# All eight heads of the second attention between the gating unit's tiles, and the gates in four wide groups

## What is computed

```python
h = rms_norm(x, norm_g)
q, k, v, z_a, u_b, v_b, z_b, g_a, g_b = split(h @ w_in)   # 7 x 1024 columns, then 2 x 2048
q, k = rms_norm(q per head), rms_norm(k per head)         # 8 heads of 128
att = causal softmax attention(q, k, v)                   # all 256 tokens are one block
y_a = (att * silu(z_a)) @ w_proj_a
mixed = w_s @ rms_norm(gelu(v_b) per head) + b_s          # 8 groups of 128, chunks of 128 tokens
y_b = (gelu(u_b) * mixed * silu(z_b)) @ w_proj_b
out = x + (sigmoid(g_a) * y_a + sigmoid(g_b) * y_b) @ w_out
```

## Time and profile before

| what | us |
|---|---|
| median of 3 runs | 1755.94 (1755.17 to 1756.29) |
| the profiled execution, its own time | 1755.48 |
| its span, first to last instruction | 1753.7 |
| u's and z_b's tiles, z_a's tiles with four heads, narrow gates with four heads | 1255.9 to 1452.8 |
| three wide gate groups | 1452.8 to 1576.7 |

### The profile page before, as it was taken

How to read it: one execution, slowest core, us unless ns; L and a number is a source line. 1 busy time by engine, 2 the same in 40 slices (tenths; PEclk the granted TensorE clock), 3 DMA queues, 4 the chain that set the end, 5 groups by cost and what they waited for, 6 DMA issues and landing times.

```text
span 1753.7 us, 24199 instructions
## 1 busy us (share of the span) xinstructions
PE 1748.2 (100%) x8722; PEld 1483.7 (85%) x8722; DVE 1391.1 (79%) x1824; ACT 941.6 (54%) x1292; POOL 234.6 (13%) x308
## 2 busy tenths in 40 slices
PE   9999999999999999999999999999999999999999
PEld 8888888888888888888888887888888888888887
DVE  6557777556799779978987887999889779995798
ACT  7434444446555445644654555767644556654454
POOL 1123434111000200110011000020102120000000
PEclk9999999999999999999999999999999999999999
DMA  9787777886767986798688776686655545666566
GB/s 326 253 272 220 228 231 218 263 268 186 248 211 233 264 258 215 230 272 246 212 231 270 242 229 227 192 252 208 205 189 178 165 163 176 212 210 198 178 199 192
DMA packets 109882, 393.33 MB, mean 224 GB/s; under 512 B 13376, under 2 KB 14032, under 8 KB 108496
## 3 DMA queue, kind: packets, MB, share of 16 engines
q1 hardware_dynamic: 93536, 333.23, 56.6%
q0 software_dynamic: 15392, 58.48, 14.5%
q10 hardware_dynamic: 864, 0.44, 0.1%
HBM read 381.60 MB, written 46.94 MB: 244 GB/s over the span
## 4 chain that ended last, share of the span: by engine, by line
PE 98%; DVE 1%; POOL 0%; ACT 0%; issue 0%; POOLq 0%; DVEq 0%
PE bank L525 23%; PE bank L546 21%; PE bank L530 12%; PE bank L840 12%; PE bank L842 12%; PE bank L841 12%; PE bank L562 1%; PE bank L596 1%; PE bank L675 1%; PE bank L718 1%; PE bank L733 1%; PE bank L724 0%; DVE w_lo L1774 0%; PE bank L717 0%; PE bank L734 0%; PE bank L646 0%
## 5 line engine op out<-in xcount | busy, mean ns | idle before, releaser
L1774 DVE TENSOR_TENSOR w_lo<-raw,w_hi 128x1024 fp32r<-128x1024 f32 x620 | 750.9, 1227 | 247.5 <-ACT w_hi L1178 244.5
L1178 ACT ACTIVATE w_hi<-raw 128x1024 fp32r<-128x1024 f32 x620 | 647.7, 1055 | 460.6 <-PE bank L546 156.2
L525 PE MATMUL bank<-h_both,w_hi 128*128 128x512 f32 x1792 | 433.5, 394 | 0.0
L525 PEld LDWEIGHTS bank<-h_both,w_hi 128*128 128x128 f32 x1792 | 330.6, 188 | 65.5
L530 PEld LDWEIGHTS bank<-h_both,w_lo 128*128 128x128 f32 x1792 | 229.8, 191 | 8.7
L530 PE MATMUL bank<-h_both,w_lo 128*128 128x256 f32 x1792 | 232.5, 283 | 0.0
L546 PE MATMUL bank<-w_hi,a_both 128*128 128x512 f32 x576 | 178.3, 391 | 0.0
L546 PE MATMUL bank<-w_hi,h_both 128*128 128x512 f32 x520 | 163.0, 394 | 0.0
L840 PE MATMUL bank<-w_hi,h_both 128*128 128x512 f32 (+1 forms) x342 | 132.8, 388 | 0.0
L842 PE MATMUL bank<-w_lo,h_both 128*128 128x512 f32 (+1 forms) x342 | 132.2, 387 | 0.0
L841 PE MATMUL bank<-w_hi,h_both 128*128 128x512 f32 (+1 forms) x342 | 132.2, 387 | 0.0
(11 more groups left out here) (317 smaller groups left out, 2370.4 us busy)
## 6 DMA issues: line engine op xcount, KB each, us to landing
raw<-in_stream SPq DMA_DIRECT2D x565, 512.0 KB, 4.3
summed<-in_stream POOLq DMA_DIRECT2D x57, 512.0 KB, 8.0
raw<-summed SPq DMA_DIRECT2D x57, 512.0 KB, 4.3
summed<-in_stream POOLq DMA_DIRECT2D x57, 256.0 KB, 7.1
wide<-scaled POOLq DMA_DIRECT2D x21, 256.0 KB, 5.1
res<-in_x SPq DMA_DIRECT2D x4, 512.0 KB, 8.0
rowg<-in_norm_rows POOLq DMA_DIRECT2D x2, 1024.0 KB, 9.5
gate<-cum_rows POOLq DMA_DIRECT2D x1, 2048.0 KB, 8.9
```

The costliest lines, as they stand in the source:

```text
L525: pe.matmul(tile_sum[b][:, :], w_hi[:, slot + half, k * P:(k + 1) * P], h_both[:, 8 * half + k, :], start=half == 0 and k == 0, stop=False)
L1178: nc.scalar.activation(w_hi[:, slot, :], raw[:, slot, :], ACT.Copy).then_inc(hi_ready, 1)
L1774: nc.vector.tensor_tensor(w_lo[:, slot, :], raw[:, slot, :], w_hi[:, slot, :].bitcast(F32), ALU.subtract).then_inc(lo_ready, 1)
```

## The change

Every head now has three tiles in the order u, z_b, z_a (`HEAD_TILES_UZ = 3`), and all eight heads run in one loop over them. Each buffer that was kept for eight groups (`u_gelu`, `za_silu`) shrinks to one. TensorE's order in a head is: tile u, `turn_probs` of the head before, `mix`, tile z_b, `weigh_values` of the head before, `turn_qk`, tile z_a, `scores`. The mix moves to banks 2 and 3. All gates are wide groups, four of them; the first starts right after the last `scores`. They use the x forms that were made for q, k and v: the low parts stay where they are, and ScalarE copies the high parts out of `a_both` in the first gate group. Until then those forms occupy blocks 9 to 12 of `a_both`, so the gating unit's results for groups 1 to 4 (`LATE_SGU`) wait in `sgu_late` and are split into hi and lo during the first gate group. GpSimd sums four more chunks. The loops over tiles are written out.

```diff
-EARLY_HEADS = 4
+HEAD_TILES_UZ = 3
+LATE_SGU = (1, 2, 3, 4)
-GATE_WIDE = 3
-GATE_NARROW = 2
+GATE_WIDE = 4
...
-        proj_bank = [bank[0:2], bank[2:4]]
-        o_bank = [[bank[0], bank[1], bank[4], bank[5]], [bank[2], bank[3], bank[6], bank[7]]]
-        o_seven = [[bank[2], bank[7], bank[3], bank[6]], [bank[0], bank[5], bank[1], bank[4]]]
-        half_bank = bank[0:2]
+        o_bank = [[bank[2], bank[3], bank[4], bank[5]], [bank[0], bank[1], bank[6], bank[7]]]
+        o_seven = [[bank[0], bank[7], bank[1], bank[6]], [bank[2], bank[5], bank[3], bank[4]]]
+        half_bank = bank[2:4]
-        mix_bank = bank[6:8]
+        mix_bank = bank[2:4]
```

TensorE's queue:

```diff
+            for h in range(MOBA_HEADS):
                 n = FOX_HEADS + h
+                uz_tile(h, 0)
                 if h:
                     turn_probs(n - 1)
+                else:
+                    pe.wait_ge(w_s_ready, 1)
+                    pe.wait_ge(join_step, 8 * GATES_FIRST)
+                mix(h)
+                uz_tile(h, 1)
                 if h:
                     weigh_values(n - 1)
+                turn_qk(n)
+                uz_tile(h, 2)
                 scores(n)
-            for i in range(GATE_NARROW):
-                if i == 1:
-                    for b in range(2):
-                        pe.wait_ge(tile_taken[b], TILES_BEFORE["gates"] // 2 + 1)
-                gate_group(i)
             for i in range(GATE_WIDE):
                 gates_group(i)
```

ScalarE's queue:

```diff
+            for h in range(MOBA_HEADS):
                 n = h + FOX_HEADS
+                tile = HEAD_TILES_UZ * h
+                c = FIRST["sgu_uz"] + 2 * tile
+                b = tile % 2
                 next_split(c)
+                act.wait_ge(uz_scaled, tile + 1)
+                nc.scalar.activation(uz_a[b], uz_x[b], ACT.Square).then_inc(uz_sq, 1)
                 next_split(c + 1)
+                if h:
+                    keep_probT(n - 1)
+                act.wait_ge(uz_cube, h + 1)
+                nc.scalar.activation(uz_b[b], uz_a[b], ACT.Tanh, scale=GELU_SCALE).then_inc(uz_tanh, 1)
+                next_split(c + 2)
+                next_split(c + 3)
                 act.wait_ge(qk_turned, h + 1)
                 nc.scalar.activation(q_head[:, :], qk_bank[:, 0:TOK], ACT.Copy,
                                      scale=hscale[:, 0:1]).then_inc(q_ready, 1)
                 if h:
+                    moba_att_hi(n - 1)
+                uz_tanh_of(tile + 1)
+                if h not in LATE_SGU:
+                    act.wait_ge(sgu_f, h + 1)
+                    nc.scalar.activation(a_hi[:, h + 8, :], uz_a[1 - b], ACT.Copy).then_inc(sgu_hi, 1)
+                next_split(c + 4)
+                next_split(c + 5)
                 exps(n)
+                uz_tanh_of(tile + 2)
...
             for j in range(WIDE_CHUNKS):
                 wide_split(GATES_FIRST, j, gate_forms[0], g_seven[0])
+                if j < STEPS:
+                    if j == STEPS - 1:
+                        act.wait_ge(logit_ready, MOBA_LAST + 1)
+                    nc.scalar.activation(g_x_hi[j], qkv_forms.x_hi[j].bitcast(F32), ACT.Copy).then_inc(x_form_ready, 1)
...
+                if 6 <= j < 6 + len(LATE_SGU):
+                    g = LATE_SGU[j - 6]
+                    act.wait_ge(sgu_f, g + 1)
+                    nc.scalar.activation(a_hi[:, g + 8, :], sgu_late[:, j - 6, :], ACT.Copy).then_inc(sgu_hi, 1)
```

VectorE's queue:

```diff
+            def sgu_lo(g, src, n):
+                dve.wait_ge(sgu_hi, n)
+                nc.vector.tensor_tensor(a_lo[:, g + 8, :], src, a_hi[:, g + 8, :].bitcast(F32),
+                                        ALU.subtract).then_inc(sgu_ready, 1)
+            for h in range(MOBA_HEADS):
...
                 next_rest(c)
+                scale_tile(b, c, tile)
+                dve.wait_ge(uz_sq, h + 1)
+                nc.vector.tensor_scalar(uz_b[b], uz_a[b], GELU_CUBE, 1.0, ALU.mult, ALU.add).then_inc(uz_step, 1)
+                dve.wait_ge(uz_step, h + 1)
+                nc.vector.tensor_tensor(uz_a[b], uz_b[b], uz_x[b], ALU.mult).then_inc(uz_cube, 1)
                 next_rest(c + 1)
+                dve.wait_ge(mix_done, h + 1)
+                for t in range(NT):
+                    nc.vector.scalar_tensor_tensor(out=mixed[:, t * P:(t + 1) * P],
+                                                   in0=mix_bank[h % 2][:, t * P:(t + 1) * P], scalar=hscale[:, 2:3],
+                                                   in1=b_s[:, h, :], op0=ALU.mult,
+                                                   op1=ALU.add).then_inc(mixed_ready, 1)
+                dve.wait_ge(uz_tanh, tile + 1)
+                nc.vector.scalar_tensor_tensor(out=u_gelu, in0=uz_b[b], scalar=1.0, in1=uz_x[b], op0=ALU.add,
+                                               op1=ALU.mult).then_inc(u_ready, 1)
+                next_rest(c + 2)
+                if h:
+                    moba_gated(n - 1)
+                scale_tile(z, c + 2, tile + 1)
+                dve.wait_ge(mixed_ready, 2 * h + 2)
+                dve.wait_ge(u_ready, h + 1)
+                nc.vector.scalar_tensor_tensor(out=mixed, in0=mixed, scalar=0.25, in1=u_gelu,
+                                               op0=ALU.mult, op1=ALU.mult).then_inc(mixed_u, 1)
+                next_rest(c + 3)
+                dve.wait_ge(uz_tanh, tile + 2)
+                nc.vector.scalar_tensor_tensor(out=uz_b[z], in0=uz_a[z], scalar=1.0, in1=uz_x[z],
+                                               op0=ALU.add, op1=ALU.mult).then_inc(zb_silu, 1)
+                dve.wait_ge(zb_silu, h + 1)
+                dve.wait_ge(mixed_u, h + 1)
+                late = h in LATE_SGU
+                sgu_out = sgu_late[:, LATE_SGU.index(h), :] if late else uz_a[z]
+                nc.vector.tensor_tensor(sgu_out, uz_b[z], mixed, ALU.mult).then_inc(sgu_f, 1)
+                if h:
+                    moba_att_lo(n - 1)
                 dve.wait_ge(q_ready, n + 1)
                 nc.vector.tensor_scalar(k_head[:, :], qk_bank[:, TOK:2 * TOK], hcols[:, 1:2], None,
                                         ALU.mult).then_inc(k_ready, 1)
+                if not late:
+                    sgu_lo(h, sgu_out, h + 1 if h == 0 else h - len(LATE_SGU) + 1)
+                next_rest(c + 4)
                 soften(n, mask)
+                scale_tile(b, c + 4, tile + 2)
+                next_rest(c + 5)
                 normalise(n)
+                dve.wait_ge(uz_tanh, tile + 3)
+                nc.vector.scalar_tensor_tensor(out=za_silu, in0=uz_a[b], scalar=1.0, in1=uz_x[b], op0=ALU.add,
+                                               op1=ALU.mult).then_inc(za_ready, 1)
             for i in range(GATE_WIDE):
+                for q in range(GROUP_STEPS[GATES_FIRST + i]):
                     wide_step(GATES_FIRST + i, q, gate_forms[i],
                               (lambda t, n: gates_drain(i - 1, t, n)) if i and q == 0 else None)
+                    if i == 0 and q == 0:
+                        moba_gated(MOBA_LAST)
+                    if i == 0 and q == 1:
+                        moba_att_lo(MOBA_LAST)
                     if i == 0 and q == 2:
+                        for k, g in enumerate(LATE_SGU):
+                            sgu_lo(g, sgu_late[:, k, :], MOBA_HEADS - len(LATE_SGU) + k + 1)
```

GpSimd's queue:

```diff
-            sum_chunks(32 + 7 * (FF_GROUPS - 1), FIRST["qkv"], (18, 22, 26, 30))
+            sum_chunks(32 + 7 * (FF_GROUPS - 1), FIRST["qkv"], range(18, 50, 4))
...
+            pool.wait_ge(qkv_in, 8)
+            scale_qk(0)
+            pool.wait_ge(qkv_in, 4 * QKV_WIDE)
+            rows_by_head(vb_head[1], vb, vb_rstd, 1).then_inc(vb_head_ready, 1)
+            for h in range(MOBA_HEADS):
+                if h + 2 < MOBA_HEADS:
+                    pool.wait_ge(mixed_ready, 2 * h + 2)
+                    rows_by_head(vb_head[h % 2], vb, vb_rstd, h + 2).then_inc(vb_head_ready, 1)
+                if h:
                     pool.wait_ge(pv_done, h + FOX_HEADS)
                 nc.gpsimd.tensor_copy(v_head[:, :, :],
+                                      qkv[:, :, h * P + 2048:(h + 1) * P + 2048]).then_inc(v_head_ready, 1)
+                if h + 1 < MOBA_HEADS:
+                    pool.wait_ge(qk_turned, h + 1)
+                    scale_qk(h + 1)
```

More of the change, by code:

```diff
@@ L79 @@
 WIDE_FIRST = [FIRST["mlp"] + 32 * (w // 2 + 1) + 32 * (w // 2) + 16 * (w % 2) for w in range(WIDE_GROUPS)]
-for _name, _at, _n in (("qkv", 16, QKV_WIDE), ("gates", GROUP_CHUNKS * GATE_NARROW, GATE_WIDE), ("out", 0, OUT_WIDE)):
+for _name, _at, _n in (("qkv", 16, QKV_WIDE), ("gates", 0, GATE_WIDE), ("out", 0, OUT_WIDE)):
     WIDE_FIRST += [FIRST[_name] + _at + WIDE_CHUNKS * i for i in range(_n)]
@@ L987, in before_seven @@
                     elif j == steps_of(w)[0][1]:
-                        pe.wait_ge(gate_taken[1], 2)
+                        for b in range(2):
+                            pe.wait_ge(tile_taken[b], TILES_BEFORE["gates"] // 2 + 1)
                         pe.wait_ge(probT_ready, MOBA_LAST + 1)
```

(25 more changed lines are left out.)

266 lines of the change are left out of this document (46 added, 220 removed).

## The result

The changed kernel takes **1758.38 us** (median of 20 runs, 1756.59 to 1759.54) where the kernel before, beside it, takes 1755.94 (20 runs, 1755.17 to 1756.47): a ratio of 1.0013, 95% interval 1.0007 to 1.0019. That lies inside the 0.2% which the prediction calls no change, and at the top edge of its range. But it is 2.4 us up where 1.6 down was forecast, and the interval leaves 1 out. So 4 us have to be found.

The account below looks back on a forecast made before the run. The prediction took TensorE's work list to bound the kernel. -3.0 for the list and stalls of +0.75, +0.3 and +0.3 sum to -1.65 us: 1753.8 for the profiled execution, median 1754.3, range 1752.5 to 1758.6.

Parts of the forecast that it names:

- The list loses 3.0 (2.7 to 3.3): TensorE's work list: twelve products removed (2.72 us) and heads in a cheaper place; shrinks by 2.7 to 3.3, taken as 3.0.
- the cheaper place of the heads: TensorE's list: four heads move from between narrow gate chunks to between tiles, 0.08 us cheaper each, 0.3 in all.
- k_head and turn_probs, 0.4 us of slack each: VectorE's two deadlines in a head, k_head before scores and normalise before turn_probs: each met with 0.4 us left.
- (3): In the heads, VectorE and GpSimd overlap and slow each other: +0.3 us, bounds 0 and 7.
- (1): Head 0: VectorE starts late and has the full list, so scores and turn_probs wait: +0.75 us, bounds 0 and 1.6.
- (2): Gate group 0: VectorE's rest of chunk 12 comes later behind the late splits: +0.3 us, bounds 0 and 1.
- Rival C: Heads 1 to 7: GpSimd blocks VectorE, k_head and probabilities come late, 6.7 us lost, 1761.0; chance 0.14.
- At nothing: the first mix and the banks of proj and out: First mix's banks are free 0.6 us ahead of need; proj and out banks keep their distances: no cost.
- At nothing: the four more summed chunks: GpSimd's queue, paced some 10 us apart in the qkv stage, is some 45 us ahead of the first mix: no cost.
- D: In the heads, an in-between case: 0.2 to 0.7 us lost a head, 1755.5 to 1759; chance 0.16.
- A: The forecast itself: tenths lost in head 0, gate group 0 and the heads' overlap, 1753.5 to 1755.3; chance 0.50.
- B: No stall anywhere, TensorE gains the whole 3.0 us: 1752.9; chance 0.20.

Follow-up runs that it names:

- `vb_first`: The changed kernel with GpSimd's vector work of the gating unit back ahead of the four added sums, at 1168 us; 1758.47 us, 1.0013 of before.
- the copies alone: The changed kernel with the added sums' whole-chunk copies left beside k's group and their accumulating transfers in heads 1 to 4; 1756.94 us, 1.0006 of before.
- the kernel with the early k_head: The changed kernel with its four added sums in heads 1 to 4 and head 0's k_head ahead of tile 1's half-sum; 1755.22 us, 0.9996 of before.
- The halved bursts: The changed kernel, added sums still beside k's and v's groups, each next copy issued two chunks after the accumulating transfer; 1756.79 us, 1.0006 of before.
- the last kernel: The changed kernel, eight sums in the heads, GpSimd's head 0 work held until k_head, four late rests in the second gate group; 1754.10 us, 0.9989 of before.

## Why the prediction was right in its stage and wrong in its total

- **What bounds the kernel.** Right, and it is why the miss was possible: with no wait left, anything that delays a load shows at once.
- **The list loses 3.0 (2.7 to 3.3).** Right. The 12 instructions are gone, the head takes 19.27 us as worked out. From v's end to the gates' end the changed kernel is 1.40 shorter with 1.24 lost in head 0 and 0.31 in gate group 0, where before lost 0.11: 1.40 + 1.24 + 0.20 = 2.84; with the tenth by which head 1 is longer than the others (19.37 and 19.27), 2.94. Less the 2.72 of the products, 0.1 to 0.2 are left for the cheaper place of the heads, not 0.3.
- **k_head and turn_probs, 0.4 us of slack each, and (3) +0.3 for heads 1 to 7.** The walk through one head was right: the trace has no wait of TensorE in any of the seven. (3) was 0.1 in head 1 and 0 in the others.
- **(1) Head 0, +0.75 (0 to 1.6).** Mis-sized: 1.24, all at the scores, where 0.5 there and 0.25 at turn_probs were forecast. The term left out is GpSimd's overlap, 0.77, the very thing that (3) put into the wrong heads. In the other heads the two engines overlap too (in head 3 two products take 0.54 and 0.51 us, not 0.42), and TensorE doesn't wait: there is slack, in head 0 there is none. The two deadlines are one, too: what is lost at the scores isn't lost again at turn_probs.
- **(2) Gate group 0, +0.3.** Measured +0.2, at the chunk named. Right.
- **Sum of the stage.** -3.0 + 0.75 + 0.3 + 0.3 = -1.65 forecast, -1.40 measured. The closeness is in part luck: head 0 cost 0.5 more than forecast, and (2) and (3) together 0.3 less.
- **Rival C's "no row shows VectorE held by more than 0.1".** The rows shown don't, but the trace of before does: the rest at 1167.40 takes 2.90 us beside GpSimd's triangle of w_s (1.37 us long). In q's group TensorE had the cover for it. No head holds such an operation, so C fell all the same.
- **At nothing: the first mix and the banks of proj and out.** Right: the mix starts at 1265.15 without a wait, and no new wait stands behind the gates.
- **At nothing: the four more summed chunks.** This is the step that failed. The prediction looked at their queue, GpSimd's, and at the distance to the first mix, and found both free. It did not ask what they carry: 3.15 MB read and as much written, from memory to memory, beside k's and v's loads. Four starts were lost there, 3.7 us by the trace: three large ones from loads that landed late, and 0.43 from GpSimd's vector work, which the sums in its queue pushed beside VectorE's. By the medians it is 2.55 us when the four go to the heads, and 3.83 when q's four go with them. The trace of before had the row that asks for it: the DMA share of q's stretch, where four such sums run, is 0.81, that of k's and v's 0.64. No rival had a place for it; D's range covers the time, not its cause.

Of the rivals, A was right as to the stage; B fell with head 0's 1.24, and C fell. What was wrong was the place where the prediction stopped looking, some 70 us ahead of the first changed product.

## What to carry to other kernels

A transfer that nobody waits for is not free where the loads of the same stage are only just in time. Count its bytes against the DMA share of the stage where it is issued, and ask how late a load may land there; moved to a stage with a lower share (here 0.49) the same transfers cost no start of TensorE. The share alone isn't a rule: q's group lost nothing at 0.81, k's lost 1.5 us at 0.72. A change that adds preparatory work should be read from the stage in which that work runs, however far it is from the lines that the change is about. And before a step is pulled forward to meet one deadline, look which engine is short: if its list is as long as before, the next deadline takes what the first one gave.

## What the runs showed of the hardware

- Loads of 512 KB in 1180 to 1215 us land in 4.2 us from the stream and 4.3 for a summed chunk (medians of the kernel before, nothing lost), in 5.6 and 7.1 beside the added sums (3.7 us lost) and in 5.4 and 6.0 in the kernel before with its sums late (2.2 lost). The median does not put the losses in order: `vb_first` lost 3.4 us at 4.8 and 7.1, the copies alone 1.5 at 4.2 and 4.6, and the kernel with the early k_head 1.4 at 4.2 and 4.3. VectorE's longest wait for one load in k's group orders them better: 0.45 us with nothing lost, 0.69 with 0.5 (the four added sums in the heads), 1.17 with 1.5 (copies alone), 1.48 with 1.4 (early k_head), 3.2 to 3.4 with 2.2 to 3.7. The halved bursts don't fit: 0.48, and 3.0 lost later, behind ScalarE's waits for loads.
- The loads get longer beside GpSimd's transfers, but neither queue is held up whole: in 1180 to 1215 us of the changed kernel the loads' queue has 48.3% of the DMA engines' time and GpSimd's 31.3%. The Trainium skill, page DMA: Bandwidth & Descriptors, section "Queues, rings and completion order", has each DMA engine go round the queues that have work, a packet at a time; the trace agrees in that both queues move on together, though it does not show the turns. Whether the loads wait in the engines or at the memory behind them, no run here separates.
- Pushed harder, the sums don't raise the DMA share of q's stretch: it stays at 0.84, and a copy there takes 8.7 us where it took 7.6.
- VectorE and GpSimd side by side stretch each other, by how much depends on the pair. In head 0 VectorE's operations grow by a sixth to a half (rest 1.22 to 1.42, products of 256 columns 0.42 to 0.50, one 0.62), and GpSimd's pair of scalings from 0.76 to 1.85 us. Beside GpSimd's triangle of w_s (1.37 to 1.39 us) a rest takes 2.53 us in the changed kernel, 2.66 in `vb_first` and 2.90 in the kernel before. The Trainium skill, page SBUF — State Buffer, section "Who interferes with whom", calls the port pair that VectorE's second input and GpSimd's reads share an exclusive lock, with the order of issue deciding who blocks. The triangle agrees with the lock: 1.22 + 1.39 = 2.61 us, with 2.53 to 2.90 measured. It does not agree with the order: in all three traces the rest starts first (in the kernel before 0.44 us ahead), and it is the rest that is long. The 1.42 of head 0 is less than a rest held for one whole scaling would take (1.22 + 0.38), and GpSimd pays more there.
- Single executions scatter more where transfers meet: 1755.17 to 1756.47 before (20 runs), 1756.59 to 1759.54 after (20), 1753.47 to 1754.74 in the last kernel (11). It is no sure sign: the kernel before spreads over 2.1 us in two of its series of 33, and the kernel with all eight sums in the heads over 2.3 in 11 runs.
